# Two-step MLP slabs, another order of loads, both cross softmaxes beside the value projection, and norms signalled by half

## The reference

```python
for l in range(DEPTH):                                   # DEPTH = 2
    h = rms_norm(x, ln_mix_pre[l]); z = h @ w_in[l]
    ...                                                  # NSA, retention, RWKV-7, short convolution
    gates = sigmoid(z_gate).reshape(B, S, 4, D_MODEL)
    merged = sum(gates[:, :, m] * (branches[m] @ w_branch[l, m]) for m in range(4))
    x = x + rms_norm(merged @ w_mix_out[l], ln_mix_post[l])
    h = rms_norm(x, ln_xa_pre[l]); mn = rms_norm(mem, ln_mem[l])
    x = x + rms_norm(cross_attention(h, mn, xa_wq[l], xa_wkv[l], xa_wo[l]), ln_xa_post[l])
    h = rms_norm(x, ln_mlp_pre[l])
    x = x + rms_norm(square(relu(h @ mlp_w1[l])) @ mlp_w2[l], ln_mlp_post[l])   # 1024 -> 4096 -> 1024
```

## Time and profile before

| | us |
|---|---|
| median of 3 runs | 2954.49 |
| lowest, highest | 2952.13, 2954.73 |
| the profiled execution | 2953.55 |
| its span | 2951.8 |
| PE busy in it | 2822.8 |

### The profile page before, as it was taken

The page is one execution under the profiler, slowest core; times in us unless marked ns, Lnnn a source line. Parts: engine busy times, 40 slices in busy tenths (PEclk is TensorE's granted clock), DMA queues, the critical chain, the costliest instruction groups (busy, mean ns, idle before and its releaser), DMA issues.

```text
span 2951.8 us, 37901 instructions
## 1 busy us (share of the span) xinstructions
PE 2822.8 (96%) x16440; PEld 2090.3 (71%) x16440; DVE 971.3 (33%) x1730; ACT 389.8 (13%) x786; POOL 90.8 (3%) x130
## 2 busy tenths in 40 slices
PE   7999998999999999899998999989999999999998
PEld 6689775666678867576676787556776776776765
DVE  2554112666355311276654773230001001001001
ACT  1230111101222111100132111210000000000000
POOL 0011200000001120000000000000000000000000
PEclk9999999999999999999999999989999999999999
DMA  5231342444333133244343443339999999999995
GB/s 229 93 143 72 136 150 86 164 171 172 107 128 122 72 126 145 106 154 168 136 145 141 158 163 123 114 141 394 373 367 365 380 355 362 386 351 370 377 387 230
DMA packets 59195, 617.19 MB, mean 209 GB/s; under 512 B 6800, under 2 KB 7056, under 8 KB 8976
## 3 DMA queue, kind: packets, MB, share of 16 engines
q1 hardware_dynamic: 56880, 603.27, 53.0%
q0 software_dynamic: 2144, 11.45, 1.0%
HBM read 613.64 MB, written 1.05 MB: 208 GB/s over the span
## 4 chain that ended last, share of the span: by engine, by line
PE 84%; DVE 8%; DMA 5%; ACT 1%; issue 1%; SPq 0%; DVEq 0%; ACTq 0%
PE ps L695 15%; PE ps L1444 14%; PE ps L1025 8%; PE ps L1454 7%; PE ps L1464 6%; PE ps L1138 6%; PE ps L1150 5%; PE ps L1005 4%; PE ps L1484 3%; DMA slabA<-in_mlp_w 3%; DVE work L1972 2%; PE ps L1037 2%; PE ps L736 2%; PE ps L676 2%; DVE work L1969 1%; PE ps L1116 1%
## 5 line engine op out<-in xcount | busy, mean ns | idle before, releaser
L1444 PEld LDWEIGHTS ps<-work,slabA 128*128 128x128 f32 x3584 | 404.4, 192 | 45.2 <-issue 45.2
L1444 PE MATMUL ps<-work,slabA 128*128 128x128 f32 x3584 | 415.0, 277 | 0.9 <-issue 0.9
L1025 PE MATMUL ps<-hT,slabA 128*128 128x256 f32 x1024 | 232.3, 380 | 1.1 <-ACT work L1703 1.1
L695 PE MATMUL ps<-hT,slabA 128*128 128x256 f32 x992 | 221.4, 384 | 2.6 <-DMA slabA<-in_od_w_in 1.5
L1025 PEld LDWEIGHTS ps<-hT,slabA 128*128 128x128 f32 x1024 | 192.2, 190 | 28.3 <-ACT work L1703 1.9
L695 PEld LDWEIGHTS ps<-hT,slabA 128*128 128x128 f32 x992 | 189.3, 192 | 29.9 <-DMA slabA<-in_od_w_in 1.7
L1454 PE MATMUL ps<-fbT,work 128*64 128x256 f32 x1792 | 207.4, 384 | 1.9 <-DMA fbT<-in_od_exp_w 1.9
L1464 PE MATMUL ps<-slabB,work 128*128 128x512 f32 x448 | 202.0, 594 | 0.0
L1454 PEld LDWEIGHTS ps<-fbT,work 128*64 128x64 f32 x1792 | 124.4, 138 | 86.6 <-issue 27.8
L2735 DVE TENSOR_TENSOR work<-work,ps 128x256 f32<-128x256 f32 x56 | 23.6, 421 | 489.5 <-ACT work L1942 489.5
L1138 PEld LDWEIGHTS ps<-work 128*128 128x128 f32 x1152 | 139.5, 192 | 21.5 <-issue 21.0
(11 more groups left out here) (385 smaller groups left out, 3092.0 us busy)
## 6 DMA issues: line engine op xcount, KB each, us to landing
slabA<-in_od_exp_w SPq DMA_DIRECT2D x56, 2048.0 KB, 9.5
fbT<-in_od_exp_w SPq DMA_DIRECT2D x56, 2048.0 KB, 10.0
slabB<-in_od_exp_w SPq DMA_DIRECT2D x56, 1024.0 KB, 8.4
fbT<-in_od_exp_w SPq DMA_DIRECT2D x56, 1024.0 KB, 10.7
slabA<-in_w_in SPq DMA_DIRECT2D x24, 2048.0 KB, 7.9
slabA<-in_mlp_w SPq DMA_DIRECT2D x32, 1024.0 KB, 6.8
slabB<-in_mlp_w SPq DMA_DIRECT2D x32, 1024.0 KB, 4.8
slabA<-in_ev_ffn_w SPq DMA_DIRECT2D x11, 2048.0 KB, 10.5
```

The lines of the kernel that those rows point to most:

```text
L695: last = mm(ps[0:rows, g % PROJ, c0:c0 + n], lhs(k), rhs(k), start=(k == 0), stop=(k == KD - 1))
L1025: last = mm(ps[:, b, 0:T], side["gates"][:, k, c % 4 * P:(c % 4 + 1) * P], hT[:, k, :], start=(k == 0), stop=(k == KD - 1))
L1444: last = mm(ps[:, 0, (2 * w + j) * P:(2 * w + j + 1) * P], v[:, k, j * P:(j + 1) * P], xs[:, k, :], start=(k == 0), stop=(k == KD - 1))
```

## The change

- The MLP's up weights are laid out so that one slabA load (2 MB) brings two steps. `ffn_step` becomes `ffn_steps`, one loop over n: in the MLP it loads a slabA for n even and then slabB(n - 1); in the gated FFN it loads slabA(n) and then slabB(n - 2).
- PE and DVE take the half of the slab that belongs to the step.
- The last two units of the merge compute both gates and then both branches, and the wait for the sums moves into `rows_out`, column by column.
- Cross attention: both tiles' scores come first, each tile has its own buffers, both softmaxes are placed beside the value projection, then both tiles' transposes, then both products with the values; one wait ahead of the output projection.
- `hT_ready` is raised for each half of the features, and PE takes the second half ahead of k = 4 in its first group or step.

```diff
+def in_twos(w):
+
+    return np.ascontiguousarray(w.reshape(-1, 2, P, KD * STEP).transpose(0, 2, 1, 3)).reshape(-1, P, 2 * KD * STEP)
...
-    o["mlp_w1"] = np.stack([stepped(w) for w in f["mlp_w1"]])
+    o["mlp_w1"] = np.stack([in_twos(stepped(w)) for w in f["mlp_w1"]])
...
+        def cross_S(t):
+            return U(14 * t)
+
+        def cross_PT(t):
+            return U(14 * t + 1)
...
-            def ffn_step(i, gated, w13, w2, last=None):
-                ringA.load(sp, [((lambda s: s[:, 0:w13.shape[1]]), w13)], ("hidden_psum", 2) if i < plain_steps(gated) else ("up_products", 2 * (1 + gated)))
-                ringB.load(sp, [(whole, w2)], last)
+            def ffn_steps(steps, gated, w13, w2, last=None):
+
+                for n in range(steps + 1 + gated):
+                    if n < steps and gated:
+                        ringA.load(sp, [(whole, w13[n])], ("hidden_psum", 2) if n < plain_steps(gated) else ("up_products", 4))
+                    elif n < steps and n % 2 == 0:
+                        ringA.load(sp, [(whole, w13[n // 2])], ("hidden_psum", 4) if n < plain_steps(gated) else ("up_products", 4))
+                    if n > gated:
+                        i = n - 1 - gated
+                        ringB.load(sp, [(whole, w2[i])], last if i == steps - 1 else None)
...
-                for i in range(FF1 // STEP):
-                    ffn_step(i, False, a["mlp_w1"][l, i], a["mlp_w2"][l, i], ("rows_psum", 2) if i == FF1 // STEP - 1 else None)
+                ffn_steps(FF1 // STEP, False, a["mlp_w1"][l], a["mlp_w2"][l], ("rows_psum", 2))
...
-            for i in range(FF2 // STEP):
-                ffn_step(i, True, a["ev_ffn_w13"][i], a["ev_ffn_w2_2"][0, i])
+            ffn_steps(FF2 // STEP, True, a["ev_ffn_w13"], a["ev_ffn_w2_2"][0])
...
-            def take_hT(tiles=NT):
-                pe.wait_ge(sem("hT_ready"), due("pe", "hT_ready", tiles))
+            def take_hT(halves=2 * NT):
+                pe.wait_ge(sem("hT_ready"), due("pe", "hT_ready", halves))
...
-                        for lhs, rhs, rows, c0, n in pieces:
+                        for p, (lhs, rhs, rows, c0, n) in enumerate(pieces):
                             for k in range(KD):
+                                if g == first and p == 0 and k == KD // 2:
+                                    take_hT(1)
...
+                            if column is not None and not t and not half:
+                                column(k)
...
-                side_units(4 * KD - side["unit"])
-                pe.wait_ge(sem("side_gate"), due("pe", "side_gate", PROJ))
-                pe.wait_ge(sem("side_summed"), due("pe", "side_summed", 4 * KD))
-                rows_out(merged)
+                side_units(4 * KD - 2 - side["unit"])
+                for u in range(4 * KD - 2, 4 * KD):
+                    side_gate(u)
+                for u in range(4 * KD - 2, 4 * KD):
+                    side_branch(u)
+                side["unit"] += 2
+
+                def merged_columns(k):
+
+                    if k == 0:
+                        pe.wait_ge(sem("side_summed"), due("pe", "side_summed", 4 * KD - 3))
+                    if k >= KD - 3:
+                        pe.wait_ge(sem("side_summed"), due("pe", "side_summed"))
+                    if k == KD - 1:
+                        pe.wait_ge(sem("side_gate"), due("pe", "side_gate", PROJ))
+                rows_out(merged, column=merged_columns)
...
-                def cross_scores(t):
-
+                for t in range(NT):
                     for h in range(4):
                         for c in range(2):
-                            last = mm(banks(0 if t else 4, 2)[:, h * T:(h + 1) * T], xq[:, 2 * h + c, t * P:(t + 1) * P], xk[:, 2 * h + c, :], start=(c == 0), stop=(c == 1))
+                            last = mm(banks(4 + 2 * t, 2)[:, h * T:(h + 1) * T], xq[:, 2 * h + c, t * P:(t + 1) * P], xk[:, 2 * h + c, :], start=(c == 0), stop=(c == 1))
                     last.then_inc(sem("scores"), up("scores"))
-                cross_scores(0)
+                for half in range(2):
+                    s = ringA.take(pe)
+                    for n in range(NT):
+                        group([rowsof(s, 512, 0, 512, n, src=memg)])
                 for t in range(NT):
-                    if t == 0:
-                        for half in range(2):
-                            s = ringA.take(pe)
-                            for n in range(NT):
-                                group([rowsof(s, 512, 0, 512, n, src=memg)])
-                    softmax_T(T)
-                    if t == 0:
-                        pe.wait_ge(sem("cross_inputs"), due("pe", "cross_inputs"))
-                        cross_scores(1)
-                    else:
-                        pe.wait_ge(sem("cross_out"), due("pe", "cross_out"))
-                    PT = U(1)
+                    pe.wait_ge(sem("weights_ready"), due("pe", "weights_ready"))
+                    for q in range(8):
+                        last = tr(banks(4 + 2 * t, 2)[:, q * P:(q + 1) * P], cross_S(t)[:, q * P:(q + 1) * P], P)
+                    last.then_inc(sem("weightsT_psum"), up("weightsT_psum"))
+                pe.wait_ge(sem("cross_inputs"), due("pe", "cross_inputs"))
+                for t in range(NT):
+                    pe.wait_ge(sem("weightsT_ready"), due("pe", "weightsT_ready"))
                     for c in range(KD):
                         for s2 in range(NT):
-                            last = mm(banks(4, 2)[:, c * P:(c + 1) * P], xv[:, s2, c * P:(c + 1) * P], PT[:, (c // 2 * 2 + s2) * P:(c // 2 * 2 + s2 + 1) * P],
+                            last = mm(banks(2 * t, 2)[:, c * P:(c + 1) * P], xv[:, s2, c * P:(c + 1) * P], cross_PT(t)[:, (c // 2 * 2 + s2) * P:(c // 2 * 2 + s2 + 1) * P],
                                       start=(s2 == 0), stop=(s2 == 1))
                     last.then_inc(sem("cross_out_psum"), up("cross_out_psum"))
-                pe.wait_ge(sem("cross_out"), due("pe", "cross_out"))
+                pe.wait_ge(sem("cross_out"), due("pe", "cross_out", NT))
...
+                                if (i, j, w, k) == (0, 0, 0, KD // 2):
+                                    take_hT(1)
...
-                slabs_at = (ringA.taken + begun, ringB.taken)
+                slabs_at = (ringA.taken, ringB.taken)
+                taken = []
+
+                def up_slab(i):
+
+                    if gated or i % 2 == 0:
+                        taken.append(ringA.take(pe))
+                    return taken[-1] if gated else taken[i // 2][:, 2048 * (i % 2):2048 * (i % 2 + 1)]
                 slabs = []
...
-                take_hT(1)
+                take_hT(2)
...
+                for half in range(2):
+                    for n in range(NT):
+                        if n == 0:
+                            act.wait_ge(sem("exp_in"), due("act", "exp_in"))
+                            nc.scalar.activation(cross_S(half), cross_S(half), ACT.Exp).then_inc(sem("exp_out"), up("exp_out"))
+                            act.wait_ge(sem("exp_out"), at("exp_out"))
+                        nc.scalar.activation(xv[:, n, 512 * half:512 * (half + 1)], take(), ACT.Copy).then_inc(sem("proj_free"), up("proj_free"))
+                        act.wait_ge(sem("proj_free"), at("proj_free"))
...
-                        done = "hT_ready" if half else "dve_order"
-                        v.tensor_tensor(d, p, gain[:, 4 * half:4 * half + 4].unsqueeze(2).broadcast_to([P, 4, P]), ALU.mult).then_inc(sem(done), up(done))
-                        dve.wait_ge(sem(done), at(done))
+                        v.tensor_tensor(d, p, gain[:, 4 * half:4 * half + 4].unsqueeze(2).broadcast_to([P, 4, P]), ALU.mult).then_inc(sem("hT_ready"), up("hT_ready"))
+                        dve.wait_ge(sem("hT_ready"), at("hT_ready"))
...
-                    s = loaded(ringA, slab + i - begun)
+                    s = loaded(ringA, slab + i) if gated else loaded(ringA, slab + i // 2)[:, 2048 * (i % 2):2048 * (i % 2 + 1)]
...
-                    softmax(T, (D // 4) ** -0.5, None, b=0 if t else 4)
+                    S3 = cross_S(t).rearrange("p (h s) -> p h s", h=4)
+                    dve.wait_ge(sem("scores"), due("dve", "scores"))
+                    ts(S3, banks(4 + 2 * t, 2).rearrange("p (h s) -> p h s", h=4), (D // 4) ** -0.5, None, ALU.mult)
+                    red(stat[:, 16 + 4 * t:20 + 4 * t], S3, ALU.max)
+                    v.tensor_tensor(S3, S3, stat[:, 16 + 4 * t:20 + 4 * t].unsqueeze(2).broadcast_to([P, 4, T]), ALU.subtract).then_inc(sem("exp_in"), up("exp_in"))
+                    dve.wait_ge(sem("exp_in"), at("exp_in"))
+                for t in range(NT):
+                    S3 = cross_S(t).rearrange("p (h s) -> p h s", h=4)
+                    dve.wait_ge(sem("exp_out"), due("dve", "exp_out"))
+                    red(stat[:, 16:20], S3, ALU.add)
+                    V(v.reciprocal(stat[:, 24:28], stat[:, 16:20]))
```

(15 more changed lines are left out.)

12 lines of the change are left out of this document (3 added, 9 removed).

## The result

The changed kernel takes 3028 us (median of 4 runs, 3020 to 3033) where the kernel before takes 2954 (4 runs, 2952 to 2955): 1.0249 times as long, 95% interval 1.0225 to 1.0272. That is 74 us more, where 78 were forecast. The profiled execution took 3032.99 us, the longest of the four; its span is 3031.2.

A forecast was written before the change was run, and what follows sets the result against it. PE, busy 96% of the span, was taken as the bound. On 2953.55 us, 134.5 more in the gated FFN and 56.4 less elsewhere gave 78 more: 3031 us, stated range 3005 to 3055.

The forecast's parts named there:

- Gated FFN, forecast +134.5: Gated FFN: slabB a step late stalls PE at nine down-product starts; 104.8 + 9.9 + 19.8 (clock) = 134.5 us more.
- Rival (a), the small load overtakes: Gated FFN: 1 MB slabB lands 4.7 us after issue despite 2 MB ahead; 52 us less, 2979; chance 0.07.
- Rival (b): Gated FFN: the late slabB is absorbed and the kernel gets faster, 2897 us; chance 0.05.
- Rival (c): MLP steps keep their waits and the clock takes 4 us a gated stall: 3063 us; chance 0.08.
- Merge, forecast 9.0: End of the merge: PE's 2.8 us wait and 1.7 us of slow matmuls go; 4.5 a layer, 9.0 us less.
- Cross, forecast 22.8: Cross attention, first scores to output projection: 42.0 us in place of 53.4; 11.4 a layer, 22.8 us less.
- Norms, forecast 6.6: Norm columns by half: each of PE's waits shrinks by 0.73 us, nine of ten count; 6.6 us less.
- MLP, forecast 15.6 and 2.4: MLP: steady steps lose their waits, 7.8 us a layer, 15.6 less; the start's second-slab wait gains 2.4.
- A slab of two steps is issued at the same place, but is first wanted a step later: MLP steady steps: 3 MB land within about 11 us and the slab is wanted 13 us after issue, so no wait.

The follow-up runs named there:

- one-line repair: The changed kernel with the gated FFN's slabB issued one step behind slabA, not two: 2897.5 us, 0.9812 of the kernel before.
- its opposite on the kernel before: The kernel before with only the gated FFN's loads in the changed order, slabA(n) then slabB(n - 2): 3086.4 us, 1.0455 of the kernel before.
- the kernel with 13 fillers: The changed kernel with 13 zero matmuls ahead of the gated down products in eight of nine stalls: 3014.2 us, 1.0203 of the kernel before.

## Why the prediction was right, and where not

**Gated FFN, forecast +134.5: right, by three terms that were each somewhat off.** The mechanism (SP's queue holds slabB behind the wait of slabA, for a whole step) is what the one-line repair and its opposite on the kernel before show. The steady stall was put at 13.1 and is 12.4 (99.0 over eight), since slabB landed in 9.7 us, not in the 10.5 of the earlier trace rows; the first was put at 9.9 and is 11.14 - 1.79 = 9.35. The clock was put at 2.2 a stall. From the start of the down products to the next four is 1651.11 - 1643.93 = 7.18 us, and 1569.76 - 1565.29 = 4.47 at full clock in the repaired kernel: 2.7. Over the nine starts the stretch is 6.30 to 7.40 us, so the cost is 1.8 at the first and 2.9 at the last, 23.8 in all, not 19.8. Sum 99.0 + 9.35 + 23.8 = 132.2. That this is within 3 us of the forecast is partly luck: the waits were put 6.4 too high and the clock 4.0 too low. The 10.5 was read where PE was at work; in the stalls PE stands idle, and there the slab came in 9.7 (more on this in the last section). The rule of the Trainium skill that I weighed there ("TensorE: Matmul & The Clock Gate", Part 1: the clock rises again only under sustained work, after a number of slow matmuls that varies) agrees with these rows, and with the cross part, where the same 32 records took 6.67 us in one kernel and 5.46 in another.

**Rival (a), the small load overtakes, failed.** In the changed kernel slabB behind 2 MB took 9.7 us, and 4.8 when it went first; the step between the two is worth 49 us. The rule of the Trainium skill ("DMA: Bandwidth & Descriptors", section "Queues, rings and completion order") that a later descriptor may finish first did not make the small load early. In both orders the load that was issued first landed first. The 1 MB took 4.8 us with the 2 MB behind it, no more than alone, and 9.7 behind them; the 2 MB took 7.6 when first and 9.4 when second. **Rival (b)**, that the gated FFN absorbs it, failed with the first stall. **Rival (c)** had the clock's direction right (2.6 on average, not 4) and its MLP wrong.

**Merge, forecast 9.0: right.** The wait (2.8 start to start) and the 1.77 of slow matmuls are gone in both layers, 9.1; undone, the time rises by 10.

**Cross, forecast 22.8: right by the rows of before (22.9), 16 to 20 by the runs.** 42.0 us, as was worked out.

**Norms, forecast 6.6: right.** All ten waits for the columns shrank by 0.73, 7.3 in all. But at the one that was said to have no slack behind it (layer 1, first tile) the wait of 0.44 for the second tile's rows came up in its place, and the stretch as a whole is 0.8 shorter, not 1.46: 6.6 are left.

**MLP, forecast 15.6 and 2.4: right, with a condition that went unsaid.** The rows give 8.6 and 8.3 in the two layers (layer 1: 155.6 us before, 147.2 after), together 16.9, and 3.0 at the start; the run says 18.6. The step "A slab of two steps is issued at the same place, but is first wanted a step later" is what the trace shows: issued right behind a slabB, wanted 12.9 us later (13 in the prediction), landed in 9.3 (11). What the prediction doesn't say is that the place stays the same only because slabB moves back by one. With the large slab alone the same queue makes the kernel 76 us slower than with both, and with the move alone slabs of one step gain 15 of the 18.6: then slabA no longer waits for the down products. The difference between slabs of one and two steps in the new order, 3.5 us, is about what the start gives, and too small to be told from none by the time alone. I had asked what the new loop does to SP's queue in the gated FFN, and did not ask the same of the MLP.

The gains by the rows are 9.1 + 22.9 + 16.9 + 3.0 + 6.6 = 58.5; with 132.2 that gives +73.7, and the medians differ by 73.8. The profiled executions, from which the rows come, differ by 79.4; 4.6 of the other 5.7 are the slow matmuls of the even layer shown above, and 1 is not accounted for. So the agreement to 0.1 us is chance.

## What to carry to other kernels

A queue that waits in order makes every load late that stands behind a wait, so in a reordering of loads ask for each one not how far ahead it is in the program, but which wait it now stands behind and when that wait ends. One place further back may cost nothing (0.980 against 0.981 of the time before) and the second 134 us, because the edge is where a wait for the step in hand comes ahead of a load for the same step. And where two edits come together (size and order), a forecast for both can be right while it says nothing of either alone: here one alone gains 15 of 18.6 us, and the other alone makes the kernel 76 us slower than both together. Only the four corners show it.

## What the hardware showed that was not expected

A stall's clock cost grows far more slowly than its length in these runs, and it is not the same each time. After 11.1 to 12.8 us of idle it was 1.8 to 2.9 us (2.6 on average), after 5.7 to 7.4 us 1.4 to 3.0 (1.9), and behind fillers with 2.2 to 2.5 us of idle 1.7 in four cases of five and nothing in the fifth. After 1.3 to 1.5 us it was nothing each time. In the even layer an idle of 3.1 us stands in all 14 kernels, ahead of the same 16 records. In one profile of each, they took 3.72 us in six kernels, 5.41 in three and 6.6 to 6.8 in five.

The 1 MB slab that stands behind 2 MB landed after 9.7 us (median) in the kernels whose PE stands idle meanwhile, the changed one and the one before with the late order. It took 10.2 to 10.6 (medians) where PE is at work, in the repaired kernel and in those with fillers, and 10.5 in the earlier trace rows. But three of the eight in the kernel with 13 fillers took 9.8 to 10.0. What links the two stays open.
